# First mixer's local attention: channel-major values product with spread and turned reciprocals

## The reference, cut to what matters

```
logits = einsum('bkgncd,bknsd->bkgncs', qb, kb) * dh**-0.5 + bias      # |i-j| <= 128, blocks of 128
m      = maximum(max(logits), sink)
p      = exp(logits - m)
denom  = sum(p) + exp(sink - m)
o      = einsum('bkgncs,bknsd->bkgncd', p / denom, vb)                 # back to [token, 8 heads x 64]
```

## Time and profile before

| what | value |
|---|---|
| three runs | 1073.91, 1075.99, 1076.28 us; median 1075.99 us |
| the profiled execution's own time | 1073.67 us |
| its span in the profile | 1071.9 us |
| PE busy | 1015.9 us, 95% of the span |
| DVE busy | 573.9 us, 54% |
| ACT busy | 400.9 us, 37% |
| the 16 units' stretch | from about 75 to 180 us of the span |

### The profile page before, as it was taken

How to read it: one execution, slowest core, us unless ns; L and a number is a source line. 1 busy time by engine, 2 the same in 40 slices (tenths; PEclk the granted TensorE clock), 3 DMA queues, 4 the chain that set the end, 5 groups by cost and what they waited for, 6 DMA issues and landing times.

```text
span 1071.9 us, 12615 instructions
## 1 busy us (share of the span) xinstructions
PE 1015.9 (95%) x5136; PEld 813.0 (76%) x5136; DVE 573.9 (54%) x760; ACT 400.9 (37%) x644; POOL 62.8 (6%) x53
## 2 busy tenths in 40 slices
PE   3899999999999999999999999989899999998997
PEld 2677767788888888888888887867768886676786
DVE  4436765435744243335324474456653857889863
ACT  3324654045633334124114354333454721212441
POOL 2300201000000000000000000003000100000300
PEclk9999999999999999999999999998999999999999
DMA  6551102024222243222322223322032356655121
GB/s 211 72 145 59 54 7 68 13 102 160 94 79 79 79 144 131 78 79 81 144 91 79 79 86 102 138 79 79 1 108 78 118 154 156 180 140 174 36 78 79
DMA packets 63359, 104.82 MB, mean 98 GB/s; under 512 B 3973, under 2 KB 27398, under 8 KB 63174
## 3 DMA queue, kind: packets, MB, share of 16 engines
q1 hardware_dynamic: 61184, 101.50, 29.1%
q10 hardware_dynamic: 2118, 2.52, 1.8%
HBM read 99.43 MB, written 4.58 MB: 97 GB/s over the span
## 4 chain that ended last, share of the span: by engine, by line
PE 77%; DVE 6%; ACT 2%; issue 2%; DVEq 0%
PE acc L737 22%; PE acc L738 22%; PE acc L739 21%; PE psT L896 2%; PE ps L1028 2%; DVE wlr L1796 1%; PE psT L1114 1%; PE psT L1013 1%; PE psT L875 1%; PE acc L1002 1%; ACT wh L1400 1%; PE acc L1094 1%; PE psT L1107 1%; PE ps L896 1%; DVE rt L1823 0%
## 5 line engine op out<-in xcount | busy, mean ns | idle before, releaser
L1796 DVE TENSOR_TENSOR wlr<-wl,wh 128x2048 fp32r<-128x2048 f32 (+1 forms) x66 | 145.2, 2203 | 77.8 <-ACT wh L1400 77.8
L737 PE MATMUL acc<-act_hi,wh 128*128 128x512 f32 x464 | 184.7, 398 | 0.3 <-DVE wlr L1796 0.3
L739 PE MATMUL acc<-act_hi,wlr 128*128 128x512 f32 x464 | 181.6, 391 | 0.0
L738 PE MATMUL acc<-act_lo,wh 128*128 128x512 f32 x464 | 181.5, 391 | 0.0
L1400 ACT ACTIVATE wh<-wl 128x2048 fp32r<-128x2048 f32 (+1 forms) x68 | 124.3, 1832 | 58.8 <-DMA wl<-in_w_up_dram 35.3
L737 PE MATMUL acc<-wh,act_hi 128*128 128x512 f32 (+1 forms) x352 | 133.6, 380 | 1.6 <-DVE act_lo L1840 1.6
L739 PE MATMUL acc<-wh,act_lo 128*128 128x512 f32 (+1 forms) x352 | 130.5, 371 | 0.0
L738 PE MATMUL acc<-wlr,act_hi 128*128 128x512 f32 (+1 forms) x352 | 130.3, 370 | 0.0
L737 PEld LDWEIGHTS acc<-act_hi,wh 128*128 128x128 f32 x464 | 87.8, 189 | 23.1 <-issue 4.2
L739 PEld LDWEIGHTS acc<-act_hi,wlr 128*128 128x128 f32 x464 | 87.5, 189 | 18.8
L738 PEld LDWEIGHTS acc<-act_lo,wh 128*128 128x128 f32 x464 | 87.8, 189 | 17.4
(11 more groups left out here) (219 smaller groups left out, 1379.9 us busy)
## 6 DMA issues: line engine op xcount, KB each, us to landing
wl<-in_w_up_dram SPq DMA_DIRECT2D x16, 1024.0 KB, 6.5
wl<-in_w_down_dram SPq DMA_DIRECT2D x16, 1024.0 KB, 6.4
wl<-in_c_w_in_dram SPq DMA_DIRECT2D x20, 512.0 KB, 5.0
raw<-in_w_in_dram SPq DMA_DIRECT2D x18, 512.0 KB, 5.4
shifted<-glu_dram SPq DMA_DIRECT2D x32, 262.0 KB, 4.7
wl<-in_a_w_in_dram SPq DMA_DIRECT2D x8, 1024.0 KB, 6.3
wl<-in_w_out_dram SPq DMA_DIRECT2D x4, 1024.0 KB, 6.4
wl<-in_ab_w_out_dram SPq DMA_DIRECT2D x4, 1024.0 KB, 8.4
```

The costliest lines, as they stand in the source:

```text
L737: pe.matmul(dst, hi, x_hi, start=first, stop=False)
L738: pe.matmul(dst, hi, x_lo, start=False, stop=False)
L739: return pe.matmul(dst, lo, x_hi, start=False, stop=last)
L1796: dve.tensor_tensor(wlr[slot][:, kk, cols], wl[slot][:, kk, cols], wh[slot][:, kk, cols].bitcast(F32), ALU.subtract).then_inc(wlo_done, 1)
```

## The change

It replaces the `pv` step of the first mixer and drops its `turn` steps. The second mixer keeps its form, with its counts of `o_done` now from zero.

- On PE the values are now the weights (64 columns), and the turned exponentials move (128 columns). Head j goes to partitions 64j to 64j+63 of `ps6`, that is to one column half of the array; the two heads alternate. The result is channel-major.
- DVE's reciprocal writes each row sum's reciprocal 64 times over (`rden`, 128x128, two buffers). PE turns this tile into `ps7[:, 0:128]`, ACT copies it to `rdenT`, and DVE multiplies `ps6` by `rdenT` straight into `o1`.
- PE's step now begins with waits for the spread reciprocals (`rden_done`) and for `ps7`.

```diff
@@ attention_unit
-            steps += [("turn", (k - 2) // 4)] if k >= 5 and k % 4 == 1 else []
+            steps += [("turn", (k - 2) // 4)] if layer == 1 and k >= 5 and k % 4 == 1 else []
@@ gla_sum
-                elif h == 0:
+                else:
                     pe.wait_ge(kst_done, 4)
-                else:
-                    pe.wait_ge(o_done, 4)
+                    pe.wait_ge(vatok_done, 4)
+                    pe.wait_ge(oq_done, STEPS)
@@ ps7_free
-                turns, values = 4 * layer + before(layer, at, "turn"), before(layer, at, "gla_values")
+                turns, values = before(layer, at, "turn"), before(layer, at, "gla_values")
...
+                if layer == 0 and before(0, at, "pv"):
+                    pe.wait_ge(rdT_done, before(0, at, "pv"))
@@ PE, pv
+                    if layer == 0:
+                        pe.wait_ge(rden_done, k + 1)
+                        ps7_free(layer, at)
+                        pe.transpose(ps7[:, 0:P], rden[:, i % 2, :], ident[:, :]).then_inc(rdT_ps, 1)
                         for b, kb in enumerate(kbs):
-                            last = pe.matmul(ps6[:, 64 * j:64 * j + 64],
-                                             PT[layer][:, (2 * b + j) * P:(2 * b + j + 1) * P],
-                                             VTOK[layer][:, kb, 64 * g:64 * g + 64],
-                                             start=b == 0, stop=b == len(kbs) - 1)
+                            for j in range(2):
+                                last = pe.matmul(ps6[64 * j:64 * j + 64, 0:P], VTOK[layer][:, kb, 64 * g:64 * g + 64],
+                                                 PT[layer][:, (2 * b + j) * P:(2 * b + j + 1) * P],
+                                                 start=b == 0, stop=b == len(kbs) - 1)
@@ ACT
+                elif what == "pv" and layer == 0:
+                    act.wait_ge(rdT_ps, k + 1)
+                    if k >= 2:
+                        act.wait_ge(oq_done, k - 1)
+                    act.activation(rdenT[:, i % 2, :], ps7[:, 0:P], ACT.Copy).then_inc(rdT_done, 1)
...
-                    halves(o1, (4, 5), lambda e, k: e.wait_ge(o_done, 4))
+                    halves(o1, (4, 5), lambda e, k: e.wait_ge(oq_done, STEPS))
@@ DVE, pv
-                    chain.link(dve.reciprocal(sm[:, :, 3:4], sm[:, :, 2:3]))
-                    dve.wait_ge(pv_done, k + 1)
...
+                    if layer == 0:
+                        if k >= 2:
+                            dve.wait_ge(pv_done, k - 1)
+                        dve.reciprocal(rden[:, i % 2, :].rearrange("p (j d) -> p j d", j=2),
+                                       sm[:, :, 2:3].to_broadcast([P, 2, 64])).then_inc(rden_done, 1)
+                        dve.wait_ge(pv_done, k + 1)
+                        dve.wait_ge(rdT_done, k + 1)
+                        dve.tensor_tensor(o1[:, 4 + i % 4, (i // 4) * P:(i // 4 + 1) * P], ps6[:, 0:P], rdenT[:, i % 2, :],
+                                          ALU.mult).then_inc(oq_done, 1)
```

More of the change, by code:

```diff
@@ L272, in block_kernel @@
         sm1 = sA("sm1", [P, 2, 2, 4])
-        oq1 = sA("oq1", [P, 4, P])
+        rden = sA("rden", [P, 2, P])
+        rdenT = sA("rdenT", [P, 2, P])
         sink1 = sA("sink1", [P, 8])
@@ L409, in block_kernel @@
         pv_done = sem("pv_done")
+        rden_done = sem("rden_done")
+        rdT_ps = sem("rdT_ps")
+        rdT_done = sem("rdT_done")
         oq_done = sem("oq_done")
@@ L508, in kst, with attention_unit @@
             return o1[:, 2 * t + d, :].rearrange("p (b n) -> p b n", b=NBLK)
-        def attention_unit(k, work):
+        def attention_unit(k, work, layer):
             steps = [("qk", k)] if k < STEPS else []
@@ L548, in mixer1_steps @@
                         work.append((("gla_gate", "gla_decay", "gla_scaled")[(k - 4) % 3], (k - 4) // 3))
-                    steps += attention_unit(k, work)
+                    steps += attention_unit(k, work, 0)
                     k += 1
@@ L572, in mixer2_steps @@
                     work.insert(0, ("pooled", (3, 5, 8, 11).index(k)))
-                steps += attention_unit(k, work)
+                steps += attention_unit(k, work, 1)
             return steps + [("pool_out", 0)]
@@ L581, in block_kernel @@
         LG, PT, SM, SINK, BIAS = (lg1, lg2), (pT1, pT2), (sm1, sm2), (sink1, sink2), (bias1, bias2)
-        OQ = (oq1, oq2)
         QH, KH, KX, VT, VTOK, OO = (qs1, q2), (k1, k2), (k1x, k2x), (v1, v2), (v1_tok, v2_tok), (o1, o2)
-        def o_tile(layer, hp):
-            return (4 if layer == 0 else 0) + hp
         STEPS_OF = (mixer1_steps(), mixer2_steps())
@@ L673, in _ @@
             load_chunk(N_AO0, a["ab_w_out_2"][0], ((0, 0, 512),))
-            sp.wait_ge(o_done, 8)
+            sp.wait_ge(o_done, 4)
             gain(gpost[:, :], a["post_norm_2"][0], gain_in)
@@ L1025, in mixer_step_pe @@
                         pe.wait_ge(relf_sb, 1)
-                    for j in range(2):
+                    if layer == 0:
+                        pe.wait_ge(rden_done, k + 1)
+                        ps7_free(layer, at)
+                        pe.transpose(ps7[:, 0:P], rden[:, i % 2, :], ident[:, :]).then_inc(rdT_ps, 1)
                         for b, kb in enumerate(kbs):
-                            last = pe.matmul(ps6[:, 64 * j:64 * j + 64],
-                                             PT[layer][:, (2 * b + j) * P:(2 * b + j + 1) * P],
-                                             VTOK[layer][:, kb, 64 * g:64 * g + 64],
-                                             start=b == 0, stop=b == len(kbs) - 1)
+                            for j in range(2):
+                                last = pe.matmul(ps6[64 * j:64 * j + 64, 0:P], VTOK[layer][:, kb, 64 * g:64 * g + 64],
+                                                 PT[layer][:, (2 * b + j) * P:(2 * b + j + 1) * P],
+                                                 start=b == 0, stop=b == len(kbs) - 1)
+                    else:
+                        for j in range(2):
+                            for b, kb in enumerate(kbs):
+                                last = pe.matmul(ps6[:, 64 * j:64 * j + 64],
+                                                 PT[layer][:, (2 * b + j) * P:(2 * b + j + 1) * P],
+                                                 VTOK[layer][:, kb, 64 * g:64 * g + 64],
+                                                 start=b == 0, stop=b == len(kbs) - 1)
                     last.then_inc(pv_done, 1)
                 elif what == "turn":
[L1035 to L1038, removed]
+                    pe.wait_ge(gated_oq, i + 1)
                     ps7_free(layer, at)
                     for hp in range(4):
-                        last = pe.transpose(ps7[:, hp * P:(hp + 1) * P], OQ[layer][:, hp, :], ident[:, :])
+                        last = pe.transpose(ps7[:, hp * P:(hp + 1) * P], oq2[:, hp, :], ident[:, :])
                     last.then_inc(oT_done, 1)
@@ L1120, in mixer_step_pe @@
                     pe.wait_ge(mix2_in, 16 * MIX2_LOADS)
-                    pe.wait_ge(o_done, 8)
+                    pe.wait_ge(o_done, 4)
                     pe.wait_ge(vtok_done, 2)
@@ L1490, in mixer_step_act @@
                 elif what == "turn":
-                    o0 = o_tile(layer, 0)
-                    act.wait_ge(oT_done, 4 * layer + i + 1)
-                    act.activation(OO[layer][:, o0:o0 + 4, i * P:(i + 1) * P],
+                    act.wait_ge(oT_done, i + 1)
+                    act.activation(o2[:, 0:4, i * P:(i + 1) * P],
                                    ps7[:, :].rearrange("p (h n) -> p h n", h=4), ACT.Copy).then_inc(o_done, 1)
+                elif what == "pv" and layer == 0:
[3 more added lines that the diff above has]
+                    act.activation(rdenT[:, i % 2, :], ps7[:, 0:P], ACT.Copy).then_inc(rdT_done, 1)
                 elif what == "gla_values":
@@ L1530, in mixer_step_act @@
                     act.wait_ge(evac_done, E_END)
-                    halves(o1, (4, 5), lambda e, k: e.wait_ge(o_done, 4))
+                    halves(o1, (4, 5), lambda e, k: e.wait_ge(oq_done, STEPS))
                     hi(N_O0, 0)
-                    halves(o1, (6, 7), lambda e, k: e.wait_ge(o_done, 4))
+                    halves(o1, (6, 7), lambda e, k: e.wait_ge(oq_done, STEPS))
                 elif what == "pool_out":
                     act.wait_ge(wtile_done, CHUNK_END[N_GB])
-                    halves(o2, (0, 1, 2, 3), lambda e, k: e.wait_ge(o_done, 8))
+                    halves(o2, (0, 1, 2, 3), lambda e, k: e.wait_ge(o_done, 4))
                     for h in range(4):
@@ L1917, in mixer_step_dve @@
                     sm = SM[layer][:, i % 2, :, :]
-                    chain.link(dve.reciprocal(sm[:, :, 3:4], sm[:, :, 2:3]))
-                    dve.wait_ge(pv_done, k + 1)
[L1920 to L1924, removed]
+                    if layer == 0:
[7 more added lines that the diff above has]
```

(9 more changed lines are left out.)

## The result

The changed kernel took a median of 1108.7 us in five runs (1107.66 to 1114.78), against 1075.99 us before. The ratio is 1.032, 95% interval 1.03 to 1.034. The forecast was 1090.3 us with a range of 1082 to 1102: the sign was right and the size less than half of what came.

A forecast was written before the change was run, and what follows sets the result against it. PE, busy 95%, was taken to bound the kernel. Waits of 18.0 us less PE's saving of 6.7 us gave +11.3, plus 3 for the clock: +14.3 on 1073.67, then 2.3 to the median: 1090.3 us, range 1082 to 1102.

The forecast's parts named there:

- the sign: Whole program: the change makes the kernel slower, chance 0.94.
- 16.2 - 2.0: PE's values step: reciprocals late by 16.2 us over 13 units, less 2.0 us for backlog in units 5 and 11.
- unit 13: PE's values step: on time before only because PE ran at half clock; otherwise about 1.0 us late.
- my 1.2 us: Unit 7: ACT's copy of turned reciprocals queues behind other work, delaying DVE and then PE's GLA values; 1.2 us.
- I took 0.89 us for 12 passes: PE's values product: six pairs in column halves take 0.89 us instead of 1.38 us.
- the reciprocal also grows from 2 to 128 elements: DVE's spread reciprocal: +0.12 us each, from a 128x128 copy's 0.28 us; 1.6 us over 13 units.
- My rival: DVE's reciprocal is slow per element: 1.0 us more instead of 0.12, +9 us in all, 1099 us; chance 0.2.
- The clock: PE's granted clock: two more half-clock spells at 1.5 us, +3 us; bounds 0 and five spells, 8 us.
- a microsecond taken from PE's queue is gained: Stretch of 16 attention units: PE bounds it, so time taken from PE's queue shortens the program one for one.
- 6.7 us net: PE's saving: 6.2 us on products plus 2.3 us on turns, less 1.8 us for 16 new transpositions.
- The last rival: DVE's lateness is backlog: only units 0, 4 and 10 wait, 7.4 us, against 10.0 us saved; 1073.4 us; chance 0.05.
- The rival that column halves don't run at once: PE's values product: a pair takes 0.24 us instead of 0.121, 9.7 us more, 1100 us; chance 0.05.

The follow-up runs named there:

- wait_only: The kernel before, with PE's values product of the first mixer also waiting for the small 2-element reciprocal; 1104.8 us.
- no_scaling: The changed kernel without the division by the row sums: no spread reciprocal, turned tile or copy of it; 1072.8 us.
- own_place: The changed kernel with small-then-spread reciprocals made ahead of the tile's evacuation, turned with the exponentials into `psT`, no new wait at the product; 1076.1 us.
- own_place_filled: own_place with unread products in PE's four waits for the GLA values' tiles; 1073.4 us.
- early_rcp: The changed kernel with DVE's long spread reciprocal moved behind the next unit's softmax, ahead of the evacuation and GLA work; 1097.0 us.
- wait_filled: wait_only with unread products ahead of PE's wait in 11 units; 1092.2 us.
- small_filled: The changed kernel with a 2-element reciprocal plus 128-element copy, and the same unread products as wait_filled; 1095.3 us.
- filled_waits: The changed kernel with two unread products ahead of PE's wait in 13 of 16 units; 1100.5 us.
- own_place_2: own_place with DVE's reciprocals of units 8, 11 and 14 behind that step's GLA decay instead of ahead of it; 1077.3 us.
- own_place_values: own_place with the turning of the GLA values behind the product of the same step instead of ahead of it; 1071.8 us.

## Why the prediction was right or wrong

**Right: the sign and the mechanism.** PE waits for a reciprocal that DVE makes behind the evacuation or the gate. With nothing else changed, this wait is 13.5 us in wait_only's profile, against my 16.2 - 2.0 = 14.2 us; with the clock mostly kept it is 16.8 us of time. In the change's own profile it is 24.1 us. My sum gives 25.4 us there once the reciprocal's measured length is put in (16.2 - 2.0 + 1.0, and 13 x 0.787 us for the growth in place of 1.6 us). The whole sum of waits without the growth, 16.2 - 2.0 + 1.0 + 1.2 = 16.4 us, stands close to the 16.8 us, but that is partly luck: unit 13 did not wait in wait_only, and ACT's copy, my 1.2 us, isn't in that kernel.

**Right: the product.** I took 0.89 us for 12 passes and measured 0.81 us in the change; the column halves run at once. By the Trainium skill's page TensorEngine Tiling (Array Packing), section Overview, Theoretical Speedup, tiles for a dimension of 64 give up to twice the speed, which would have been 0.69 us. The trace shows 1.7 times (1.38 by 0.81), between my figure and the page's.

**Wrong: the step "the reciprocal also grows from 2 to 128 elements".** I took the copy's 0.28 us; it measured 0.944 us, 6.2 ns for each further element (0.944 less 0.157, over 126). The term stood at 1.6 us of waits; by the measured length it was 10.2 us (13 x 0.787). My rival had 1.0 us more for one reciprocal and 9 us in all; taking the short reciprocal gave back 6.5 us, and 5.2 us with the clock kept. I gave that rival 0.2, because the 2-element row seemed to speak against it. That row can't tell: by the measured rate two elements are 12 ns of 157, and the operation on 4 elements that I set beside it, at 158 ns, is of another kind. The Trainium skill's page VectorE: DVE Perf Modes, section First, the fixed hardware budget, names a repeat count of 8 for the reciprocal's iterative divide. The trace agrees in kind and not in number: 6.2 ns for each further element, less than the 7.8 ns that I estimate as eight times the copy's rate.

**Wrong: the step "The clock".** I expected two more half-clock spells at 1.5 us and gave 8 us as the upper bound. The stretch had 37.6 us more at half clock, in eight spells where one had been. Filling gave back 8.2 us in the change, with 10.2 us of half clock still left, and 12.6 us by the medians in wait_only (7.6 by the profiles), where I had put 3 us. Together with the reciprocal this puts the result outside the range: with the reciprocal short the kernel took 1102.2 us, just above the range's end, and with the clock mostly kept 1100.5 us, inside it. I had read the earlier trace rows as a rare event in a stretch with one thin spot; the change made thin spots in twelve of sixteen units.

**Wrong: the sentence "a microsecond taken from PE's queue is gained".** I took PE's 5% of idle time as room to spare on the other engines. DVE's tail at the GLA values' tiles was already PE's largest wait, and PE, with less work, ran into it. Of the 8.5 us that I had put on product and turns, no_scaling kept 2.3: it waits 1.4 us longer at these tiles and has 6.8 us more of half clock, up to 3.4 us of work. Of the 6.7 us net, own_place kept nothing and own_place_filled 1.3.

**Small misses.** Between the reciprocal's end and PE's start lie 0.2 to 0.3 us in each unit (162.34 to 162.66 in unit 9), which I left out; over 12 units that is about 3 us. The step also begins with a wait for `ps7`, which I had put at nothing; it is mostly hidden behind the long reciprocals in the change, and early_rcp, whose reciprocals are ready in all units but one, shows it: 6.4 us in seven units. DVE waited for ACT's copy, which I gave 1.2 us in unit 7 alone, twice in the change (3.4 us), and nine times in early_rcp (16.9 us), where it is DVE's longest wait.

The shares, from one run to the next: from before to wait_filled 16.8 us (waits for the small reciprocal), to small_filled 3.2 us (the new product, the turned tile and the spreading copy, what they save and what they add), to filled_waits 5.2 us (the long reciprocal), and to the change 8.2 us (the clock, with the unread products gone). Such differences in a row add up by construction, here to 33.3 us, so the sum checks nothing; and small_filled and filled_waits don't hold the same unread products. What the row shows is that the new form saved PE nothing that could be seen, where I had taken off 6.7 us.

The last rival, that the lateness is backlog and three units wait for 7.4 us, is refuted by wait_only: 11 units waited for 13.5 us. The rival that column halves don't run at once is refuted by the product's time.

## What to carry to other kernels

Before an operand is moved onto the tensor engine's path, look where in its maker's queue it is made: a result that nobody waited for may be late in every unit, and the distance from its end to the new reader's start, read in the trace of before, is the price. In a stretch like this one, many waits of one or two microseconds cost more than their sum, because the granted clock falls: in wait_only's profile 13.5 us of waits brought up to about 10 us of lost work. And if another engine's tail is the largest wait already, first move work between its result and the wait; here that alone was worth 0.35%, at least as much as all the saved passes (0.27% in no_scaling, which leaves out the division).

## What the runs showed that I had not expected

- Unread products made three kernels faster by 7 to 13 us, and own_place by 2.7 us.
- The 128-element reciprocal takes 6.2 ns for each further element, against about 1.0 ns for a copy.
- A DVE copy of 128x128 from SBUF to SBUF took 0.23 us in 15 of 16 units but 1.09 us in the one where GpSimd was multiplying; it ended within 0.1 us of GpSimd's instruction. DVE, then POOL, in own_place:

```profile
121.91 0.23 DVE L1957 COPY rden<-sm 128x128 f32<-128x128 f32 x1
...
129.49 1.09 DVE L1957 COPY rden<-sm 128x128 f32<-128x128 f32 x1
...
127.24 3.26 POOL L1298 TENSOR_TENSOR ka<-ka,sq 128x512 f32<-128x512 f32 x1
```

The same copy took 1.09 us beside the same GpSimd product in own_place_2, own_place_filled and own_place_values too. It stands right ahead of the evacuation for which PE waits 3.5 us in own_place, so some 0.86 us of that wait would be the copy's. That the one engine holds the other up is what these rows suggest; no run took it apart.
